# Delta levels that read 64 of 128 columns of the moving operand, with both growths of a group in one PSUM bank

## The reference

```python
def gated_delta_rule(q, k, v, g, beta):
    # Recurrence: S_t = a_t (S_{t-1} - beta_t k_t k_t^T S_{t-1}) + beta_t k_t v_t^T,  o_t = S_t^T q_t.
    n = l // CHUNK                                          # CHUNK = 64
    ...
    decay = jnp.exp(jnp.where(causal, g[..., :, None] - g[..., None, :], NEG_INF))
    lower = jnp.where(strict, jnp.einsum('bhncd,bhnmd->bhncm', kb, k) * decay, 0.0)
    eye = jnp.eye(CHUNK, dtype=jnp.float32)
    t_inv = lax.linalg.triangular_solve(lower + eye, jnp.broadcast_to(eye, lower.shape),
                                        left_side=True, lower=True, unit_diagonal=True)
    u = t_inv @ vb
    w = t_inv @ (kb * jnp.exp(g)[..., None])
    ...

def reference(x, c, ada_w, ...):
    x = first_block(x, c, ada_w, ...)        # attention, MLP, recurrent block, MLP
    return second_block(x, rel_bias_2, ...)  # twice: SwiGLU, hybrid_mixer, SwiGLU

def hybrid_mixer(x, w_in, conv_w, ...):
    ...                                      # windowed attention on one side
    o = gated_delta_rule(qb, kb, vb, g, beta)
    ...
    return (gate_a * ya + gate_b * yb) @ w_out
```

## Time and profile before

| | us |
|---|---|
| median of 3 runs | 2425.2 |
| lowest, highest | 2424.6, 2425.63 |
| the profiled execution, its own time | 2425.95 |
| its span in the trace | 2424.2 |
| TensorE busy in the span | 2279.1 |
| VectorE, ScalarE, GpSimd busy | 1588.8, 1140.6, 371.9 |
| all matmuls of line 883, share of the chain that ended last | 6% |

### The profile page before, as it was taken

How to read it: one execution, slowest core, us unless ns; L and a number is a source line. 1 busy time by engine, 2 the same in 40 slices (tenths; PEclk the granted TensorE clock), 3 DMA queues, 4 the chain that set the end, 5 groups by cost and what they waited for, 6 DMA issues and landing times.

```text
span 2424.2 us, 37471 instructions
## 1 busy us (share of the span) xinstructions
PE 2279.1 (94%) x15862; PEld 2092.7 (86%) x15862; DVE 1588.8 (66%) x1858; ACT 1140.6 (47%) x1533; POOL 371.9 (15%) x305
## 2 busy tenths in 40 slices
PE   3879998888799999999999999999999999999998
PEld 3768887877799899998799889989999879988997
DVE  6988776499855754669755575465556985557545
ACT  2335344288444544456642454354345665235433
POOL 2112221211300210030033030012004003302100
PEclk9889999989899999999999999999999999999999
DMA  8868883434365465664431246546565453114652
GB/s 309 274 210 277 283 274 105 141 85 110 114 218 191 156 209 189 142 194 148 112 122 53 78 155 216 187 147 221 179 174 169 145 131 105 53 67 162 212 186 104
DMA packets 304282, 400.48 MB, mean 165 GB/s; under 512 B 43215, under 2 KB 262969, under 8 KB 304116
## 3 DMA queue, kind: packets, MB, share of 16 engines
q1 hardware_dynamic: 283360, 336.75, 43.4%
q0 software_dynamic: 17504, 57.89, 7.3%
q10 hardware_dynamic: 3252, 3.45, 0.4%
HBM read 393.86 MB, written 4.19 MB: 164 GB/s over the span
## 4 chain that ended last, share of the span: by engine, by line
PE 79%; DVE 14%; ACT 4%; issue 2%; DMA 1%; SPq 0%; DVEq 0%; ACTq 0%
PE tiles L496 16%; PE tiles L497 16%; PE tiles L498 16%; PE y_rows L496 6%; PE y_rows L497 6%; PE y_rows L498 6%; PE tiles L883 6%; DVE weights_lo L1367 2%; DVE ada_acc L1417 1%; ACT weights_hi L990 1%; DMA ada_ring<-in_ada_w_dram 1%; PE tiles L596 1%; DVE rnn_r L1688 1%; PE tiles L620 1%; DVE rnn_conv_out L1657 1%
## 5 line engine op out<-in xcount | busy, mean ns | idle before, releaser
L1367 DVE TENSOR_TENSOR weights_lo<-weights_raw,weights_hi 128x2048 fp32r<-128x2048 f32 (+2 forms) x316 | 768.1, 2437 | 509.1 <-ACT weights_hi L990 508.9
L496 PE MATMUL tiles<-xt_hi,weights_hi 128*128 128x256 f32 (+1 forms) x3216 | 919.1, 286 | 22.9 <-DVE weights_lo L1367 12.4
L497 PE MATMUL tiles<-xt_lo,weights_hi 128*128 128x256 f32 (+1 forms) x3216 | 912.4, 284 | 0.0
L498 PE MATMUL tiles<-xt_hi,weights_lo 128*128 128x256 f32 (+1 forms) x3216 | 912.3, 284 | 0.0
L990 ACT ACTIVATE weights_hi<-weights_raw 128x2048 fp32r<-128x2048 f32 (+2 forms) x316 | 593.0, 1880 | 210.2 <-PE y_rows L498 178.2
L496 PEld LDWEIGHTS tiles<-xt_hi,weights_hi 128*128 128x128 f32 (+1 forms) x3216 | 612.0, 190 | 39.9 <-issue 21.5
L497 PEld LDWEIGHTS tiles<-xt_lo,weights_hi 128*128 128x128 f32 (+1 forms) x3216 | 612.4, 190 | 2.8
L498 PEld LDWEIGHTS tiles<-xt_hi,weights_lo 128*128 128x128 f32 (+1 forms) x3216 | 612.0, 190 | 0.0
L496 PE MATMUL y_rows<-weights_hi,hid_hi 128*128 128x512 f32 x608 | 241.8, 398 | 0.0
L497 PE MATMUL y_rows<-weights_lo,hid_hi 128*128 128x512 f32 x608 | 239.3, 394 | 0.0
L498 PE MATMUL y_rows<-weights_hi,hid_lo 128*128 128x512 f32 x608 | 238.8, 393 | 0.0
(11 more groups left out here) (349 smaller groups left out, 3013.2 us busy)
## 6 DMA issues: line engine op xcount, KB each, us to landing
weights_raw<-in_ffn_w_dram SPq DMA_DIRECT2D x132, 1024.0 KB, 5.0
weights_raw<-in_mlp_w_dram SPq DMA_DIRECT2D x64, 1024.0 KB, 6.1
weights_raw<-in_w_in_dram SPq DMA_DIRECT2D x52, 1024.0 KB, 5.2
ada_ring<-in_ada_w_dram POOLq DMA_DIRECT2D x76, 512.0 KB, 4.9
weights_raw<-in_rnn_w_in_dram SPq DMA_DIRECT2D x16, 768.0 KB, 4.6
ada_ring<-in_ada_w_dram SPq DMA_DIRECT2D x20, 512.0 KB, 7.2
weights_raw<-in_w_in_dram SPq DMA_DIRECT2D x32, 256.0 KB, 4.3
weights_raw<-in_w_branch_a_dram SPq DMA_DIRECT2D x32, 256.0 KB, 4.8
```

The source lines that it names most:

```text
L496: pe.matmul(o, a, c, start=first, stop=False)
L497: pe.matmul(o, a, d, start=False, stop=False)
L498: return pe.matmul(o, b, c, start=False, stop=last)
L1367: dve.tensor_tensor(slot_view(WLO, m, NSPL), slot_view(RAW, m, NRAW), slot_view(WHI, m, NSPL).bitcast(F32), ALU.subtract).then_inc(*inc("l ...
```

## The change

Levels from 2 on give the x matmul only the 64 columns of `TT` that can be filled, as a strided access pattern (`part`: columns in runs of 2^i, every second run), and the result stands packed in the first half of a bank. The growths do so from level 1 on: dt takes 64 columns of `XX`, du 64 columns of `UU`. Both growths of a group now stand in one bank, in its two halves, as one tile with one signal behind all eight matmuls. The weights of every matmul are the same 128x128 as before, and so is the number of matmuls. x of level 1 is as before.

Since only half of the columns of `XX` and `MM` are written now, rows and columns of older levels stay in them. What they would add is masked when a tile is read: ScalarE copies x with a scale for each partition that is 1 on rows of the upper halves and 0 on the others; VectorE subtracts dt over 64 columns and adds du times 0 or -1 for each partition (a scalar_tensor_tensor in place of a tensor_tensor). These factors are a new table of 128x14 (`ODD`), loaded by one more DMA of GpSimd's queue at s = 5. GpSimd's mask product covers 64 columns from level 2 on. What waits for dt before (x of the next level) now waits for du.

```diff
--- before.py
+++ after.py
@@ -89,7 +89,9 @@
     for i in range(7):
         s = 1 << i
         lv.append(((ci // (2 * s) == mi // (2 * s)) & (ci % (2 * s) >= s) & (mi % (2 * s) < s)).astype(np.float32))
+    odd = (np.arange(P)[:, None] >> np.arange(7)[None, :]) & 1
     c["levels_t"] = np.concatenate(lv, 1)
+    c["odd_rows"] = np.concatenate([odd, odd - 1], 1).astype(np.float32)
     c["row_eps"] = np.tile(np.array([[128 * NORM_EPS, NORM_EPS, 1e-30]], np.float32), (8, 1))
     return c
 
@@ -167,6 +169,7 @@
         AT1 = put("attn_small", [P, 6, 16])
         A2S = put("attn2_small", [P, 3, 8])
         GCOL = put("g_cols", [P, 6, 8])
+        ODD = put("odd_rows", [P, 14])
         EPS = put("ln_eps", [P, 1])
         gate_at = pos["at"]
         GATE = put("gate_rows", [P, D])
@@ -377,6 +380,14 @@
 
         y_end = {x[0][0]: ("rows_done", x[0]) for x in slots if x[0][1] in ("w2", "out")}
 
+        def part(m, i, odd):
+
+            return m.rearrange("p (a t b) -> p t a b", t=2, b=1 << i)[:, odd]
+
+        def parts(m, i, odd):
+
+            return m.rearrange("p c (a t b) -> p t c a b", t=2, b=1 << i)[:, odd]
+
         def slot_view(ring, n, depth):
             _, p, (a_, b_), _ = slots[n]
             return ring[0:p, n % depth, 0:a_ * b_].rearrange("p (a b) -> p a b", a=a_)
@@ -899,19 +910,33 @@
                     pe.wait_ge(*past("u0_ready", (s, g)))
                     turn4(("t0", g), "A", lambda j: UU[:, g, j, :])
                 fill = {1: ("gb", 2), 2: ("gb", 3), 3: ("ga", 0), 5: ("ga", 1)}
+
+                def halves(bank, half, i, lhs, rhs, odd):
+
+                    for j in range(4):
+                        o = bank[:, half * S + 64 * j:half * S + 64 * j + 64].rearrange("p (a b) -> p a b", b=1 << i)
+                        ins = pe.matmul(o, lhs[:, j, :], part(rhs[:, j, :], i, odd), start=True, stop=True)
+                    return ins
+
                 for i in range(1, 7):
                     for g in range(4):
                         pe.wait_ge(*past("m_ready", (s, i, g)))
-                        pe.wait_ge(*past(*(("free_A", (s, "t0", g)) if i == 1 else ("free_D", (s, "dt", i - 1, g)))))
-                        four(("x", i, g), "A", lambda j: MM[:, g, j, :], lambda j: TT[:, g, j, :])
+                        pe.wait_ge(*past(*(("free_A", (s, "t0", g)) if i == 1 else ("free_D", (s, "du", i - 1, g)))))
+                        if i == 1:
+                            four(("x", i, g), "A", lambda j: MM[:, g, j, :], lambda j: TT[:, g, j, :])
+                        else:
+                            bank = topen((s, "x", i, g), "A")
+                            halves(bank, 0, i, MM[:, g], TT[:, g], 0).then_inc(*inc("tile_done", (s, "x", i, g)))
                     if i in fill:
                         cols_slot((s,) + fill[i], XH, XL, "A")
                     for g in range(4):
                         pe.wait_ge(*past("free_A", (s, "x", i, g)))
-                        pe.wait_ge(*past(*(("u0_ready", (s, g)) if i == 1 else ("free_D", (s, "du", i - 1, g)))))
+                        if i == 1:
+                            pe.wait_ge(*past("u0_ready", (s, g)))
+                        bank = topen((s, "du", i, g), "D")
                         if i < 6:
-                            four(("dt", i, g), "D", lambda j: UU[:, g, j, :], lambda j: XX[:, g, j, :])
-                        four(("du", i, g), "D", lambda j: XX[:, g, j, :], lambda j: UU[:, g, j, :])
+                            halves(bank, 0, i, UU[:, g], XX[:, g], 0)
+                        halves(bank, 1, i, XX[:, g], UU[:, g], 1).then_inc(*inc("tile_done", (s, "du", i, g)))
                 for hf in range(2):
                     pe.wait_ge(*past("free_D", (s, "du", 6, 2 * hf)))
                     pe.wait_ge(*past("free_D", (s, "vt", 2 * hf)))
@@ -1308,7 +1333,11 @@
                 fill = {1: ("gb", 2), 2: ("gb", 3), 3: ("ga", 0), 5: ("ga", 1)}
                 for i in range(1, 7):
                     for g in range(4):
-                        four(("x", i, g), XX[:, g, :, :])
+                        if i == 1:
+                            four(("x", i, g), XX[:, g, :, :])
+                        else:
+                            bank = tile((s, "x", i, g))[:, 0:S].rearrange("p (c a b) -> p c a b", c=4, b=1 << i)
+                            evac((s, "x", i, g), parts(XX[:, g], i, 0), src=bank, scale=ODD[:, i:i + 1])
                     if i in fill:
                         gate(*fill[i])
                 for hf in range(2):
@@ -1841,14 +1870,16 @@
                     if i - 1 in fill and fill[i - 1][0] == "ga":
                         gate_a(fill[i - 1][1])
                     for g in range(4):
-                        for kind, dst in (("dt", TT), ("du", UU)):
-                            if kind == "dt" and i == 6:
-                                continue
-                            bank = tile((s, kind, i, g))
-                            m = dst[:, g, :, :]
-                            if i == 1:
-                                dve.wait_ge(*past("free_A", (s, "t0", g)))
-                            dve.tensor_tensor(m, m, bank.rearrange("p (a b) -> p a b", a=4), ALU.subtract).then_inc(*inc("free_D", (s, kind, i, g)))
+                        bank = tile((s, "du", i, g))
+                        if i == 1:
+                            dve.wait_ge(*past("free_A", (s, "t0", g)))
+                        if i < 6:
+                            m = parts(TT[:, g], i, 0)
+                            dt = bank[:, 0:S].rearrange("p (c a b) -> p c a b", c=4, b=1 << i)
+                            dve.tensor_tensor(m, m, dt, ALU.subtract).then_inc(*inc("t_grown", (s, i, g)))
+                        m = parts(UU[:, g], i, 1)
+                        du = bank[:, S:2 * S].rearrange("p (c a b) -> p c a b", c=4, b=1 << i)
+                        dve.scalar_tensor_tensor(m, du, ODD[:, 7 + i:8 + i], m, ALU.mult, ALU.add).then_inc(*inc("free_D", (s, "du", i, g)))
                 dve.wait_ge(*past("k_decay", s))
                 for hf in range(2):
                     bank = tile((s, "ks", hf))
@@ -2037,6 +2068,7 @@
 
                     if s == 5:
                         pool.dma_start(LVL[:, :], C["levels_t"]).then_inc(*inc("dn_const_in", None, 16))
+                        pool.dma_start(ODD[:, :], C["odd_rows"]).then_inc(*inc("dn_const_in", None, 16))
                         pool.dma_start(TRI[:, :], C["causal_t"]).then_inc(*inc("dn_const_in", None, 16))
                         pool.wait_ge(*past("dn_const_in"))
                     for n in range(4):
@@ -2046,7 +2078,10 @@
                     def level(i, g):
                         hf, c = divmod(g, 2)
                         lev = LVL[:, i * P:(i + 1) * P].rearrange("p (a b) -> p a b", a=1).broadcast_to([P, 4, P])
-                        pool.tensor_tensor(MM[:, g, :, :], LE[hf][:, :, c, 1, :], lev, ALU.mult).then_inc(*inc("m_ready", (s, i, g)))
+                        m, le = MM[:, g, :, :], LE[hf][:, :, c, 1, :]
+                        if i >= 2:
+                            m, le, lev = parts(m, i, 1), parts(le, i, 1), parts(lev, i, 1)
+                        pool.tensor_tensor(m, le, lev, ALU.mult).then_inc(*inc("m_ready", (s, i, g)))
                         pool.wait_ge(*past("m_ready", (s, i, g)))
 
                     pool.wait_ge(*past("row_split", s))
```

## The result

The changed kernel takes 2431.81 us (median of 10 runs, 2429.89 to 2433.85), the kernel before 2425.77 beside it (10 runs, 2424.6 to 2430.35). The ratio is 1.0023, with a 95% interval of 1.0013 to 1.0033: slower by 6 us, a little more than the 0.2% that I had set as the bound of "no change". The profiled execution took 2432.68 us with a span of 2430.9, against 2425.95 and 2424.2. So 6.7 us have come into the span, and the trace can say where.

A forecast was written before the change was run, and what follows sets the result against it. TensorE alone was taken to bound the levels, each piece paid for its weight load. 0 on the pieces and 0 for the rest left the profiled execution at 2425.95 us, the median at 2425.2; range 2420 to 2438 us.

The forecast's parts named there:

- short falls of the clock: TensorE's clock dropping briefly, as behind 288 us: +1.7 us each, one or two allowed for in the range.
- Pieces at 0.1117 us whatever their columns: Level matmuls on TensorE: 1024 pieces going from 128 to 64 columns keep 0.1117 us each, paid for weight load; 0 change.
- The lower end: One-column float32 matmuls of line 596, same 128x128 stationary tile loaded anew: 0.1106 us each at full clock.
- Strided reading 0: TensorE reading TT, UU and XX in runs of 2 to 64 elements was taken to cost 0.
- rival 3: Level matmuls: strided reads pass the weight load, slower by 13 us (level 1 alone) to 106 us; 3%.
- One signal, shorter copies, shorter masks, all covered: Level changes: VectorE's later dt start, ScalarE's scaled copies and GpSimd's masks stay hidden behind TensorE; cost 0.
- Rival 1: Level matmuls: the load isn't the bound for 64 columns, so -57.2 us, 2368 us; 7%.
- Rival 2: Level matmuls: TensorE's clock falls with 64-column pieces, +52 us (2477) or, never recovering, +103 (2528); 12%.
- The new table: One more DMA issue of 0.55 us on GpSimd's queue ahead of causal_t: cost 0, at most 0.55.

The follow-up runs named there:

- part 4: Changed kernel with its new table in a free stretch elsewhere, each of the 1024 level products moving one column instead of 64: 2518.96 us, ratio 1.0377.
- table_elsewhere: Changed kernel with its new table put into a free stretch of another area, so nothing else moves from the kernel before: 2427.08 us, ratio 0.9996.
- the experiment with 64x64: Changed kernel with its table elsewhere, the 1024 level products taking 64 stationary and 64 moving columns: 2378.41 us, ratio 0.9794.
- shift_only: Kernel before with 64 unused bytes where the change puts its new table, nothing else changed: 2432.96 us, ratio 1.0026.

## Why the prediction was right about the levels and wrong about the time

Forecast: 2425.2 us and no change, with 77%. Measured: 2431.81, slower by 0.23%. The time lies in the range of 2420 to 2438 us, but that range was drawn for other causes (strided reads, short falls of the clock), so it held by luck.

- **Pieces at 0.1117 us whatever their columns:** right. 0.1114 in the changed kernel, 0.1114 (21.39 / 192) without the shift. The reason given, the weight load, held in both experiments that aimed at it. The lower end was read a little short: 1.77 / 16 = 0.1106 averages a short first step and a long last one, and the fourteen between are 0.1116 us each; in part 4 one-column pieces at full clock stand 0.1115 apart.
- **Strided reading 0:** right. Pieces that read in runs of 2 to 64 elements are 0.111 to 0.113 us apart at every level of `table_elsewhere`, the growths of level 1 with the shortest runs 0.1109, and rival 3 is gone.
- **One signal, shorter copies, shorter masks, all covered:** right. The growths are 0.42 and 0.48 us (0.41 was forecast for the second), VectorE's idle time before a pair is 0.97 (0.95 forecast).
- **Rival 1 (faster, 2368 us):** didn't occur; the experiment with 64x64 shows what it would have taken, a smaller stationary tile.
- **Rival 2 (slower, the clock falls):** didn't occur at 64 columns, and did at one, at the price that was worked out for it.
- **The new table:** this is the step that failed. I costed it as "one more DMA issue, 0.55 us", and put 0 for it. A table also takes a place, and here the places behind it move. That term was missing. It is 1824 products times 0.2334 - 0.2279 = 0.0055 us, 10.0 us in all. The median moved by 6.0 (3 to 8 by the interval), and the two traces show what stands between. From 208 us on the products at full clock take 9.2 us longer, and TensorE's waits take none of it back. In the first 208 us the changed kernel's trace gained 1.5. The many 256-column products on `xt_*` are 0.1 ns closer together, 0.9 us in all. And the short stretches at half clock, which both traces have, fell on other matmuls: 2.2 us more on the products of `hid_*`, 2.6 us less on the 256-column products of `ot_hi` and `ot_lo`. One such stretch of before and of after, in windows:

```profile
1376.00:1382.00 6.00, 5.72 (x27) 5.75 (x28) 5.33 (x9) 3.26 (x4) 0.54 (x1) 0.50 0.07 29
```

```profile
1381.00:1384.00 3.00, 2.77 (x13) 2.80 (x14) 2.93 (x6) 0.77 (x2) 0.00 (x0) 0.50 0.10 41
```

That is why the offset between the traces did not grow from 1352 to 1600 us, although the products there were 1.2 us slower. Such stretches lie differently from trace to trace, and no experiment here was made on them.

The diff shows the line that did it, and the addresses could be worked out beforehand: by the `put` lines `hid_hi` starts 123392 bytes (482 x 256) behind `weights_hi` in the kernel before, and 123456 after the change. That an address could cost anything stood in no row of the trace of before, in which all the large products on `weights_*` have the distance 0 modulo 256. But that is itself the point: an unknown that no row shows needs a bound, and naming "moves stationary operands of 1824 products" as a term with an unknown price would have taken chance from "no change".

What stays open is why the distance counts. That two reads of the same partitions, the load of the next stationary tile and the stream of the current moving one, get in each other's way is a guess that would fit, since the effect hangs on both addresses together and came back after 256 bytes in both pairs tried (0 and 256, 128 and 384). No run here shows the reads themselves, so it is not shown. It is not seen in the level pieces either: in the changed kernel and in `shift_only` their stationary `l_level_t` lies 64 bytes off against `t_inv`, and they keep 275 ns and, with 128 columns in `shift_only`, 0.1117 us from start to start.

## What to carry to other kernels

Before counting the columns that a product can be spared, look at what sets the time from one start to the next of its kind in the profile: where one column takes as long as 128, fewer moving columns bring nothing. Here fewer stationary columns did, and thinning the stream down to one column cost the clock. And a buffer that is added in the middle of a list of addresses is an edit to all behind it: put it at the end or into a hole, and compare the durations of matmuls that the diff doesn't touch.

## What the runs showed that I had not expected

- 512-column products on float32 pairs (128 stationary columns, a load for each) take 0.2279 us when stationary and moving operand start at the same place modulo 256 bytes, and 0.2291 to 0.2334 at the four other distances tried. That is up to 2.4% of these products from nothing but placement.
- With one moving column in each level product TensorE's granted clock was 0.65 over 77 us in which it was busy 77.00, and the kernel took 92 us longer for less work.
- Halving both operands' columns nearly halves a piece (0.1117 to 0.0581 us); halving the moving ones alone does nothing.
